# Out tiles in pairing order, all weight sums of the first two gate/up pairs by adding DMA, and the next pair's first product moved last

## The reference

```python
x = x + jnp.einsum('btd,de->bte', merged, w_out[l])
h2 = rmsnorm(x, norm_ffn[l])
gu = jnp.einsum('btd,df->btf', h2, w_gate_up[l])
g, up = jnp.split(gu, 2, axis=-1)
x = x + jnp.einsum('btf,fd->btd', jax.nn.silu(g) * up, w_down[l])
```

## Time and profile before

| | |
|---|---|
| median of 3 runs | 2176.88 us (2176.58 to 2177.26) |
| the profiled execution's own time | 2173.83 us |
| its span, first to last instruction | 2172.0 us |
| PE busy | 2147.0 us (99%) |
| DVE busy | 1586.7 us (73%) |
| ACT busy | 1042.5 us (48%) |
| POOL busy | 145.5 us (7%) |
| mean granted clock of PE | 0.995 |

### The profile page before, as it was taken

One profiled execution on the slowest core, in us unless ns is written; L12 is line 12 of the kernel. 1 busy time (PEld: TensorE's weight loads), 2 busy tenths in 40 slices (PEclk: granted clock), 3 DMA queues, 4 the chain that ended last, 5 costly groups with the idle time before them and its releaser, 6 DMA issues.

```text
span 2172.0 us, 31430 instructions
## 1 busy us (share of the span) xinstructions
PE 2147.0 (99%) x12112; PEld 1860.1 (86%) x12112; DVE 1586.7 (73%) x2428; ACT 1042.5 (48%) x1705; POOL 145.5 (7%) x187
## 2 busy tenths in 40 slices
PE   9999999999999999999999999999999999999998
PEld 6888879999888887879999888888888899888887
DVE  8999978888546999978888534664766568888723
ACT  5678555555324688546555323332554344222312
POOL 0000031111000000031111000000000000000000
PEclk9999999999999999999999999999999999999999
DMA  5221216675233212226776233223232231222222
GB/s 185 74 78 67 93 63 177 187 180 160 95 111 110 86 65 80 79 77 170 192 177 164 94 108 130 97 97 115 88 107 68 97 136 59 97 97 97 88 98 76
DMA packets 52937, 239.92 MB, mean 110 GB/s; under 512 B 6432, under 2 KB 6944, under 8 KB 32352
## 3 DMA queue, kind: packets, MB, share of 16 engines
q1 hardware_dynamic: 40880, 216.92, 28.5%
q0 software_dynamic: 11520, 20.98, 6.0%
q10 hardware_dynamic: 432, 0.64, 0.1%
HBM read 232.61 MB, written 2.10 MB: 108 GB/s over the span
## 4 chain that ended last, share of the span: by engine, by line
PE 89%; DVE 6%; ACT 4%; issue 1%; DMA 0%; SPq 0%; DVEq 0%
PE mm L2197 21%; PE mm L2198 21%; PE mm L2199 21%; PE sp L2197 7%; PE sp L2199 7%; PE sp L2198 7%; DVE conv_y L1416 1%; DVE probs L1446 1%; ACT probs L705 1%; PE ob L2401 1%; ACT probs L697 1%; PE sp L2373 1%; DVE w_lo L1315 1%; PE sp L2388 0%; DVE w_lo L1636 0%
## 5 line engine op out<-in xcount | busy, mean ns | idle before, releaser
L2197 PE MATMUL mm<-in_hi,w_hi 128*128 128x512 f32 (+1 forms) x1520 | 540.0, 355 | 8.9 <-DVE act L1744 4.1
L2198 PE MATMUL mm<-in_lo,w_hi 128*128 128x512 f32 (+1 forms) x1520 | 532.6, 350 | 0.0
L2199 PE MATMUL mm<-in_hi,w_lo 128*128 128x512 f32 (+1 forms) x1520 | 532.5, 350 | 0.0
L638 ACT ACTIVATE w_hi<-w_raw 128x2048 fp32r<-128x2048 f32 (+3 forms) x145 | 256.2, 1767 | 461.3 <-PE mm L2199 343.1
L1315 DVE TENSOR_TENSOR w_lo<-w_raw,w_hi 128x2048 fp32r<-128x2048 f32 (+3 forms) x149 | 323.1, 2170 | 196.3 <-ACT w_hi L638 193.8
L2197 PEld LDWEIGHTS mm<-in_hi,w_hi 128*128 128x128 f32 x1520 | 286.7, 189 | 54.0 <-issue 13.0
L2199 PEld LDWEIGHTS mm<-in_hi,w_lo 128*128 128x128 f32 x1520 | 286.5, 188 | 38.0
L2198 PEld LDWEIGHTS mm<-in_lo,w_hi 128*128 128x128 f32 x1520 | 286.9, 189 | 36.7 <-issue 1.0
L1416 DVE SCALAR_TENSOR_TENSOR conv_y<-conv_in,parl,conv_y 128x512 f32<-128x512 f32 x240 | 169.3, 743 | 1.3
L2197 PE MATMUL sp<-in_hi,w_hi 128*128 128x512 f32 (+1 forms) x432 | 146.3, 339 | 0.0
L2199 PE MATMUL sp<-in_hi,w_lo 128*128 128x512 f32 (+1 forms) x432 | 145.7, 337 | 0.0
(11 more groups left out here) (496 smaller groups left out, 4477.1 us busy)
## 6 DMA issues: line engine op xcount, KB each, us to landing
w_raw<-in_w_dram SPq DMA_DIRECT2D x160, 1024.0 KB, 4.8
w_raw<-in_w_dram SPq DMA_DIRECT2D x32, 704.0 KB, 3.9
w_third_sum<-in_w_dram SPq DMA_DIRECT2D x40, 256.0 KB, 4.2
w_raw<-in_w_dram POOLq DMA_DIRECT2D x40, 256.0 KB, 3.7
w_third_sum<-in_w_dram POOLq DMA_DIRECT2D x40, 256.0 KB, 5.0
w_raw<-in_w_dram SPq DMA_DIRECT2D x5, 512.0 KB, 4.7
out_dram<-z_rows SPq DMA_DIRECT2D x8, 256.0 KB, 2.1
rope<-in_rope_dram SPq DMA_DIRECT2D x3, 512.0 KB, 3.4
```

What stands on the lines that cost most here:

```text
L638: e.activation(whi[:, slot, 0:cols], raw[:, slot, 0:cols], ACT.Copy).then_inc(s_whi, whi_out.up())
L2197: MM(out, ah, bh, start=first, stop=False, **kw)
L2198: MM(out, ah, bl, start=False, stop=False, **kw)
L2199: return MM(out, al, bh, start=False, stop=last, **kw)
```

## The change

The diff has five parts.

1. The out tiles are worked in the order 0, 4, 1, 5, 2, 6, 3, 7 (the weights are laid out so in memory ahead of the launch), and the token operands of a couple k, k + 4 are made right after its two tiles. The last tile is added to x in two halves.
2. The sums of pairs 0 and 1 come from adding DMAs too: SP issues two more loads of A21, and POOL issues the four adding DMAs in between its additions of squares (after the third and the fifth). w_sum and the sums on DVE and POOL go; DVE waits for the DMA on slot 1 before it takes the last out tile.
3. PE's order in a pair becomes T1(p), T4(p-1), T2(p), B21(p), T3(p), B22(p), B11(p+1). The pair's first product for the next pair is last, and one product stands between T2(p) and T3(p).
4. The waits follow the new numbering; ACT's copy_1 moves to the start of the pair, gate_takes waits for count 1 in place of 0, and in the last pair up_takes stands ahead of kept_low(0).
5. The inverse root of the norm is made inside pair 0's end; its table is loaded ahead of the out tiles. Zeroing the sum of squares moves into pair 2. PE's loop over the pairs has its first and last pair taken out.

```diff
+OUT_ORDER = (0, 4, 1, 5, 2, 6, 3, 7)
-        (wsum,) = phase(("w_sum", [P, 2, CH], F32))
...
+                for slot in range(2):
+                    e.dma_start(w3[:, slot, :],
+                                W[bass.ds(n + (gate_up + slot), 1), :, A21].rearrange("a p c -> (a p) c")).then_inc(s_w3[slot], 16)
...
+            def sums_by_dma(l, p):
+
+                a, n = p % 2, l * L_CHUNKS + GATE_UP + p
+                e.wait_ge(s_raw[a], raws[a].next(16))
+                e.dma_start(raw[:, a, A21], W[n:n + 1, :, A22].rearrange("a p c -> (a p) c"),
+                            accum_op=ALU.add).then_inc(s_a1[a], 16)
+                e.wait_ge(s_w3[a], begun[a].next(16))
+                e.dma_start(w3[:, a, :], W[n:n + 1, :, A11].rearrange("a p c -> (a p) c"),
+                            accum_op=ALU.add).then_inc(s_a3[a], 16)
...
+                    if layer is not None and k in (2, 4):
+                        sums_by_dma(layer, k // 2 - 1)
...
                 def gated_pair(p, m, split):          # ACT
 
+                    last = p == FT - 1
                     e.wait_ge(s_ds, sums.next())
-                    e.wait_ge(s_sm, done.now())
+                    e.wait_ge(s_sm, done.now(1))
                     high_of(5, raw[:, p % 2, A12])
-                    if p < FT - 1:
+                    if p > 1:
+                        copied_out(copy_1[p % 2], bank_x[p % 2], 0)
+                    if not last:
+                        e.wait_ge(s_sm, done.now())
                         landed((p + 1) % 2)
                         high_of(0, raw[:, (p + 1) % 2, A11])
                     silu()
                     third_high(p)
                     copied_out(copy_5[p % 2], bank_z[p % 2], 1)
-                    if p < FT - 1:
-                        next_weights(p)
+                    if not last:
+                        e.wait_ge(s_sm, done.now(-3))
+                        first_and_second_high(p + 1)
+                    copied_out(copy_2[p % 2], bank_x[p % 2], 3)
+                    if not last:
+                        e.wait_ge(s_sm, done.now(-4))
+                        other_highs(p + 1)
                         done.skip(7)
...
                 def gated_pair(p, m, split):          # DVE
 
-                    gate_takes(p - 1, 0)
+                    gate_takes(p - 1, 1, fn.next() if p == 1 else None)
                     low_of(5, raw[:, p % 2, A12])
                     low_of(0, raw[:, (p + 1) % 2, A11])
                     silu = fn.next()
...
-                    fourth_sum(p + 1)
-                    up_takes(p, 6, 2)
+                    fourth_sum(p + 1, raw[:, (p + 1) % 2, A11])
+                    up_takes(p, 5, 2)
...
+                fourth_sum(0, raw[:, 0, A11])
+                e.wait_ge(s_a1[1], firsts[1].next(16))
+                TT(tA[:, 0:T], raw[:, 1, A11], raw[:, 1, A21], ALU.add).then_inc(s_ds, wsums.up())
+                new_x_by_halves(KT - 1, 1)
...
             def gated_pair(p):                        # PE
...
                 times(bank_y[a], 3, B21, True)
-                if not last:
-                    e.wait_ge(s_sv, products.now(-2))
-                    operand(2)
-                    times(bank_x[1 - a], 0, B11, True)
                 e.wait_ge(s_sc, copies.now(-3))
                 operand(2 if last else 3)
                 times(bank_x[a], 4, T3, False)
                 e.wait_ge(s_sc, copies.now(-2))
                 times(bank_z[a], 5, B22, False)
+                e.wait_ge(s_sv, products.now(-3 if last else -2))
                 if last:
-                    e.wait_ge(s_sv, products.now(-3))
                     times(bank_x[a], 6 + a, T4, False)
+                else:
+                    times(bank_x[1 - a], 0, B11, True)
```

More of the change, by code:

```diff
@@ L587, in _ @@
                     q_scale()
[L588 to L598, removed]
-                for p in range(2, FT):
[L600 to L606, removed]
+                for r in raws:
+                    r.skip(16 * (GATE_UP // 2))
+                add_squares(l)
+                for p in range(2, FT):
+                    sums_by_dma(l, p)
                 for r in raws:
@@ L890, in token_high, with first_and_second_high @@
                     hi(token_operand(HIGH, o, k), src, scale)
[L892 to L903, removed]
+                def first_and_second_high(p):
+                    e.wait_ge(s_ds, sums.next())
+                    e.activation(first_and_second_sum(whi), raw[:, p % 2, 2 * OP:CH], ACT.Copy).then_inc(s_sh, high.up())
@@ L905, in _, with squared @@
+                def squared(m, d):
+                    e.wait_ge(s_sum, added.next())
+                    square(x[:, m, :], d)
+                e.preload_act_table_set(LN_EXP)
                 e.wait_ge(s_val, val.next())
-                for m in range(KT):
-                    k, g = m % HK, col(parl, A_GF + m)
+                for k in range(HK):
+                    g_k, g = col(parl, A_GF + k), col(parl, A_GF + HK + k)
                     tiles.skip(1)
[L909 to L912, removed]
@@ L927, in _ @@
[L927 to L930, removed]
+                    token_high(B11, k, x[:, k, first_half], g_k)
+                    e.wait_ge(s_val, val.next())
+                    token_high(T1, k, token_operand(SUM, T2, k), minus_g[:, k:k + 1])
+                    if k == HK - 1:
+                        first_and_second_high(0)
+                    squared(k, 0)
+                    tiles.skip(1)
@@ new lines, in _ @@
+                    if k == HK - 1:
+                        break
+                    if k < 2:
+                        prep(k)
+                    else:
+                        landed(0)
+                        e.wait_ge(s_mm, tiles.now())
+                        high_of(0, raw[:, 0, A11])
+                    e.wait_ge(s_mmf, taken.next())
+                    hi(tB[:, 0:TH], x[:, HK + k, second_half], g)
+                    token_high(B21, k, x[:, HK + k, first_half], g)
+                    sum_token_high(T2, k)
@@ L931, in _ @@
+                copied_out(copy_1[0], bank_x[0], 1)
+                sum_token_high(T2, k)
+                third_high(0)
+                sum_token_high(T3, k)
+                e.wait_ge(s_ds, sums.next())
+                high_of(5, raw[:, 0, A12])
+                copied_out(copy_2[0], bank_x[0], 3)
+                token_high(B22, k, x[:, KT - 1, second_half], g)
+                squared(KT - 1, 1)
+                copied_out(copy_5[0], bank_z[0], 2)
                 landed(1)
+                e.wait_ge(s_ds, sums.next())
@@ L932, in _ @@
+                high_of(1, raw[:, 1, A21])
+                sum_hi()
                 high_of(0, raw[:, 1, A11])
[L933 to L940, removed]
-                high_of(6, raw[:, 0, A22])
[L943 to L955, removed]
@@ L1672, in _ @@
-                e.wait_ge(s_val, val.now())
-                for m in range(HK):
-                    out_first(m)
-                    if m % 2:
-                        prep(m // 2)
-                new_x(HK)
-                out_second(HK)
-                new_x(HK + 1)
-                out_second(HK + 1)
-                low_of(0, raw[:, 0, A11])
-                TT(spot(wsum, 1), raw[:, 0, A21], raw[:, 0, A22], ALU.add).then_inc(s_ds, wsums.up())
-                e.wait_ge(s_ds, wsums.now())
@@ L1791, in _ @@
                 prep(0, HALF)
+                up_takes(FT - 1, 5, 2)
                 def kept_low(m):
```

244 lines of the change are left out of this document (133 added, 111 removed).

## The result

| | before | after |
|---|---|---|
| median, 4 runs each | 2177.07 us (2176.58 to 2178.46) | 2244.36 us (2240.15 to 2245.28) |
| the profiled execution's own time | 2173.83 us | 2244.89 us |
| its span | 2172.0 us | 2243.1 us |
| PE busy | 2147.0 us (99%) | 2157.6 us (96%) |
| mean granted clock | 0.995 | 0.994 |

The ratio of the medians is 1.0305, with a 95% interval of 1.0292 to 1.0318: 3.1% slower. The forecast was 2227 us, with a range of 2205 to 2262.

What follows compares the result with a forecast made beforehand. PE, busy 99% of the span, was taken as the bound. 2173.83 + 55.5 (settled pairs) - 6.6 (transition) + 1.0 (last pairs) = 2223.7 us profiled; the median 3.05 higher, 2226.8, range 2205 to 2262.

Steps and rivals of the forecast that it cites:

- The settled pair: Pairs 2 to 20 of each layer: each 1.46 us longer, 11.4 in place of 9.94, +55.5 us in all.
- (a): Settled pair: T3, now the fifth product, wants to start at 5.68, not 7.10; 1.2 us to spare become 0.2 missing.
- (b): Settled pair: gate_takes waits for T1(p), starting at 1.62 in place of 0.20, and moves the chain to copy_2 by 1.42.
- Rival A: Settled pairs: only the new order costs, gate_takes' wait being already satisfied; 0.30 + 0.10 a pair, 2185 us; chance 0.05.
- Rival B: Settled pairs: both delays hidden because PE takes the copy's signal within the product ahead; pairs stay 9.94, 2169 us; chance 0.06.
- Rival C: Settled pairs: PE's short idling lowers the clock; 2311 us if in every pair, 2255 in a third; chance 0.10.
- none after a single one: Argument on the clock from the earlier trace: it fell once, after two stalls, and never after a single stall.
- The transition: Change from out product to pairs: a gain of 3.3 us a layer (0.7 to 6.0), -6.6 us in all.
- landing 3.7: Transition: the adding DMA ahead of second_sum and T3(1) was taken to land 3.7 us after POOL issues it.
- The last pair: Last pair of each layer: up_takes ahead of kept_low(0) saves 0.6, its chain starts 1.42 later; +0.5 a layer, +1.0.
- The narrower range of the sum: Whole kernel: 38 x 0.15 for the pairs and the transition's bounds, added as independent, 2214 to 2240 us.

Runs made afterwards that it cites:

- e2: The changed kernel with gate_takes waiting for B22(p-1) (count -1) in place of T1(p): 2195.82 us, ratio 1.0086 to the kernel before.
- e3: The changed kernel with copy_2 ahead of the next pair's high parts on ACT, gate_takes still waiting for T1(p): 2176.79 us, ratio 1.0008 to the kernel before.
- e6: e4 with only pair 0's w_raw adding DMA after POOL's third square, the other three after the fifth: 2170.28 us; repeated on another chip 2169.98 us.
- e4: The changed kernel with both gate_takes waiting for B22(p-1) and copy_2 ahead of the high parts: 2177.19 us, ratio 1.0003 to the kernel before.
- e8: e6 with SP's load for pair 3 waiting two low parts later (operand 4 of pair 1): 2166.80 us, ratio 0.9958 to the kernel before.

## Why the prediction was right, and where not

- **The settled pair: right.** (a) and (b) and their meeting hold: gate_takes at 1.62 as forecast, second_sum's end 5.56 (5.55), copy_2's end 6.98 (6.91), T3 at 7.10 (7.04), a pair longer by 1.54 (1.46). Of the 0.08, 0.06 lie in ACT's start 0.09 after second_sum, not 0.03, and the rest in the one pair that took 11.76. On the chip (b) alone costs 0.44, at B11(p+1) and not at T3, (a) alone 0.34, and taking copy_2 from behind the high parts takes the whole away.
- **The size of (a) alone: right.** Rival A put 0.40 a pair on the order, e2 measured 0.34. Rival B's premise, that a late signal is hidden, fell: PE shows the stall in full.
- **Rival C, the clock: wrong.** PE idles 1.26 of each 11.46 us, and the clock of that stretch is 1.00 (window 350 to 541). It fell to its lower level (1.2 of 2.4 GHz) in the transitions, behind the idling of 7.94 and 7.99 us, each a single long stall, and in the second layer also behind the 2.14 us ahead of T2(0), which follow on 0.84 and 1.21 (granted clock 0.66 from 1011 to 1016). The prediction's "none after a single one" was a reading of the first layer alone: in the second layer of the kernel before the matmuls behind the stall of 2.25 at 974.22, the first one there, are slow already, and the clock from 974 to 985 is 0.54. Behind the 7.94 us, in the first layer, 23 matmuls are 0.21 apart in place of 0.12, about 2.2 us, as the earlier trace rows had shown. The rule of the Trainium skill, "TensorE: Matmul & The Clock Gate", section "A second HAM failure mode: psum-queue depth-cycling", by which short and frequent idling makes the clock swing, would have given 2255 to 2311; the trace disagrees for this rhythm.
- **The transition: the term that was mis-sized.** The earlier trace rows leaves out one more of its waits, 3.9 us for early_lo; that one is gone after the change, as the prediction wanted. Forecast -3.3 us a layer, measured +5.9 in the first (+6.2 in the second), so some 18.5 us for both layers, outside its bounds of -6.0 to -0.7. In the profiled execution the miss is 2244.89 - 2223.7 = 21.2: 18.5 here, 3.0 in the pairs (58.5 against 55.5), -0.4 in the last ones. The median missed by 17.6 only, since it lies 0.5 below the profiled time of the kernel after and lay 3.05 above that of the kernel before, which is chance and no merit of the forecast. Two steps of it failed. "I estimate that DVE takes the last tile at 316.7": it took it at 321.24, 4.5 later. The prediction saw that POOL would wait for A21, but counted only DVE's wait for the adding DMA, not the three additions that pile up meanwhile and then run beside DVE. From the tile on it was right again: 8.67 to the last low part, against 8.7. And "landing 3.7": it took 7.2, 3.5 more, because pair 3's load starts 0.4 behind. The earlier trace rows is a median over 40 DMAs, nearly all from settled pairs; the one on the path had other traffic. The stretch at half clock cost the 2.2 that the prediction had named as possible and counted by half: 4.5 + 3.5 + 1.1 is 9.1 of the 9.2 us missed in the first layer.
- **The last pair.** Forecast +0.5, measured +0.3 a layer. Its stall, 0.92, is still released by up_takes.
- **The range.** The narrower range of the sum, 2214 to 2240, was missed by 4.4 us, and its working is off: 5.7 for the pairs and 5.3 for the two transitions, added as independent, make 7.8 and not 13. The wide range, 2205 to 2262, held with the transition wrong in sign, because half of rival C had been put into it.

The forecast held because 58.5 of the 71.1 us were a chain that could be added up from three queues. Not tried: to have SP's load wait for the adding DMA itself, which would fix their order in place of leaving it to the count of products. How e3's gain in the first transition divides was not told apart either: T3(1) is no longer held, the clock no longer falls behind it (it falls behind T2(0)'s stall there, 0.66 from 322 to 327), and its load came 1.0 behind the adding DMA, which then took 4.3 and not 7.2.

## What to carry to other kernels

On a queue worked off in order, look at what stands behind the instruction that waits: a copy that frees a bank belongs ahead of the preparation of the next weights, not behind it, and then the lateness of that preparation costs nothing. When a step is moved, its producer's slack and its consumer's slack shrink together: price both edits at once, since 0.44 and 0.34 apart became 1.54 together. Put a wait into a helper engine's queue only where little work stands behind it, and take a DMA's duration from the place where it will run, not from its median.

## What the runs showed of the hardware

**POOL's additions hold DVE up.** DVE's slow operations end shortly after POOL's addition does, whatever their size: the 3.37 one at 314.42, POOL at 313.86; the 2.78 one of e6 at 311.74, POOL at 311.17; the 1.65 one at 320.71, POOL at 320.17; the 1.51 one at 311.12, POOL at 310.84. Taken from POOL's end, 0.56, 0.57, 0.54 and 0.28 are a little under their own durations (0.69, 0.69, 0.69, 0.42). That looks like waiting, not like sharing. The Trainium skill, "SBUF — State Buffer", section "SBUF: two separate sides", says so: the port pair of the two engines is an exclusive lock, and a vector operation with both inputs in SBUF waits for a GpSimd operation that reads SBUF. The trace agrees. It isn't the adding DMAs' writing: the slow operation of 1.49 in the kernel before stands at 319.85 and the first adding DMA of that layer at 333.79, and in the kernel after DVE took its usual 0.69 at 335.69 and 336.73, while one was under way. Beside the DMA issues of e6 from 307.19 on DVE ran at its usual pace too. One row stays open: the 3.37 operation started at 311.05, beside DMA issues, and at its usual length would have ended 0.2 ahead of the addition recorded at 311.94. Spans on POOL are rough, so it doesn't decide between a start recorded late and a part played by the issues.

**An adding DMA of 256 KB is slowed by a load that starts just behind it.** It took 7.2 and 7.4 us with a 1 MB load 0.4 and 0.5 us behind, 6.8 with the load 0.7 behind (e4, first layer), 4.3 with 1.0 (e3, first layer), 3.8 and 3.7 with 1.8 and 2.4, 3.8 with none. So it turns between 0.7 and 1.0 us. The row of e3, where POOL issued at 335.30 and SP at 336.28:

```profile
339.60 0.69 DVE L1692 TENSOR_TENSOR w_raw<-w_raw 128x512 f32<-128x512 f32 x1 [1.93 <-DMA w_raw<-in_w_dram]
```

This is not a matter of the transition alone. In e6 (451.75, load 0.2 behind, 7.1 us) and e8 (1041.26, load 0.3 behind, 7.3 us) it happened among the settled pairs.
